# A hybrid encoder layer on one core: the next pair's columns move to another buffer, the down sums move to slots 13 to 46, and the last passes' outputs leave their banks in two steps

## The reference

```
h = rms(x); q, k, v, c = split(h @ w_in)
attn = window_attention(rms(q), rms(k), v)          # 128-query blocks, 384-key bands
u = a * sigmoid(gate); u = silu(layernorm(dwconv31(u)))
x = x + concat(attn, u) @ w_out
h2 = rms(x)
g = silu(dwconv3(h2 @ ffn_w_gate) + b)
x = x + (g * (h2 @ ffn_w_up)) @ ffn_w_down          # the larger part of the time
```

## Time and profile before

| what | value |
| --- | --- |
| median of 3 runs | 2567.1 us (2565.86 to 2567.85) |
| profiled execution, its own time | 2563.86 us |
| its span in the trace | 2561.8 us |
| PE busy | 2519.3 us, 98% of the span |
| DVE, ACT, POOL busy | 76%, 56%, 12% |
| DMA share in 0 to 200 us, 200 to 400 us | 0.94, 0.88 |
| granted PE clock, mean | 0.995 |

### The profile page before, as it was taken

The page is one execution under the profiler, slowest core; times in us unless marked ns, Lnnn a source line. Parts: engine busy times, 40 slices in busy tenths (PEclk is TensorE's granted clock), DMA queues, the critical chain, the costliest instruction groups (busy, mean ns, idle before and its releaser), DMA issues. The chain is left out here.

```text
span 2561.8 us, 36076 instructions
## 1 busy us (share of the span) xinstructions
PE 2519.3 (98%) x12663; PEld 2242.3 (88%) x12663; DVE 1936.6 (76%) x3228; ACT 1431.1 (56%) x2578; POOL 319.8 (12%) x483
## 2 busy tenths in 40 slices
PE   8999999999999999999999999999999899999997
PEld 7877777788878888888888899999999899999997
DVE  5886767887878697969794678687687887867864
ACT  6345544468436852784474356665655665655654
POOL 1110121201011102110101101100100111011011
PEclk9999999999999999999999999999999999999999
DMA  9988988834464456445537736735746675475465
GB/s 361 387 315 313 339 329 347 305 113 169 175 236 144 148 217 244 154 152 217 203 132 295 261 98 154 174 106 132 171 108 182 145 160 127 113 170 133 111 151 108
DMA packets 166834, 505.80 MB, mean 197 GB/s; under 512 B 28832, under 2 KB 37536, under 8 KB 147200
## 3 DMA queue, kind: packets, MB, share of 16 engines
q1 hardware_dynamic: 119344, 336.60, 37.6%
q0 software_dynamic: 47312, 166.91, 24.4%
HBM read 350.07 MB, written 153.36 MB: 197 GB/s over the span
## 5 line engine op out<-in xcount | busy, mean ns | idle before, releaser
L2037 DVE TENSOR_TENSOR part_lo<-part_raw,part_hi 128x512 fp32r<-128x512 f32 x462 | 316.7, 689 | 237.1 <-ACT part_hi L1561 234.3
L2357 PE MATMUL bank<-hw_hi,weights 128*128 128x462 f32 (+3 forms) x1408 | 420.7, 373 | 0.0
L1858 DVE SCALAR_TENSOR_TENSOR cc<-win,par,cc 128x512 f32<-128x512 f32 x600 | 408.3, 744 | 0.0
L1561 ACT ACTIVATE part_hi<-part_raw 128x512 fp32r<-128x512 f32 x462 | 285.7, 628 | 176.2 <-DMA part_raw<-w_pass_t 71.1
L2308 PE MATMUL bank<-h_hi,weights 128*128 128x512 f32 x1104 | 355.6, 395 | 0.0
L2521 PE MATMUL bank<-mid,part_hi 128*128 128x414 f32 x1232 | 337.3, 354 | 13.7 <-DVE pair_y L2122 6.0
L2357 PEld LDWEIGHTS bank<-hw_hi,weights 128*128 128x128 f32 x1408 | 264.7, 188 | 37.3 <-issue 12.2
L2357 PE MATMUL bank<-hw_lo,weights 128*128 128x464 f32 (+3 forms) x704 | 259.2, 368 | 0.0
L2308 PEld LDWEIGHTS bank<-h_hi,weights 128*128 128x128 f32 x1104 | 207.9, 188 | 51.7 <-issue 6.1
L2521 PEld LDWEIGHTS bank<-mid,part_hi 128*128 128x128 f32 x1232 | 231.9, 189 | 20.5 <-DVE part_lo L2037 9.9
L2503 PE MATMUL bank<-T_hi,part_hi 128*128 128x414 f32 (+1 forms) x704 | 246.0, 349 | 2.1 <-DVE e L2061 2.1
(11 more groups left out here) (231 smaller groups left out, 4596.1 us busy)
## 6 DMA issues: line engine op xcount, KB each, us to landing
weights<-weight_scratch SPq DMA_DIRECT2D x88, 1024.0 KB, 7.3
y_pair_t<-pair_y POOLq DMA_DIRECT2D x140, 414.0 KB, 7.8
wraw<-w_ffn_t SPq DMA_DIRECT2D x88, 512.0 KB, 3.3
part_raw<-w_ffn_t SPq DMA_DIRECT2D x176, 256.0 KB, 2.8
weight_scratch<-weights POOLq DMA_DIRECT2D x22, 1024.0 KB, 8.0
wraw<-w_down_t SPq DMA_DIRECT2D x44, 512.0 KB, 3.3
part_raw<-down_sums SPq DMA_DIRECT2D x88, 256.0 KB, 4.5
part_raw<-w_pass_t SPq DMA_DIRECT2D x66, 256.0 KB, 5.9
```

The source lines that it names most:

```text
L1561: nc.scalar.activation(p_hi[k % HI_RING][:], p_raw[part_of(k)][:], ACT.Copy).then_inc(s_whi, 1)
L1858: nc.vector.scalar_tensor_tensor(acc, win[i][:, tap:tap + TB], w_tap, acc, ALU.mult, ALU.add).then_inc(s_cv, 1)
L2037: nc.vector.tensor_tensor(p_lo[part_of(k)][:], p_raw[part_of(k)][:], p_hi[k % HI_RING][:].bitcast(F32), ALU.subtract).then_inc(s_wlo, 1)
L2357: mm = nc.tensor.matmul(out, l[:, k, :], r[:, k, cols], start=(k == 0 and j == 0), stop=(k == KT - 1 and j == 2))
```

## The change

It has three parts. First, the down sums' rounds start at slots 13, 16, 19, 23, 26, 29, 33, 36, 39, 43 and 46, where before they started at 12, 16, 20 and so on to 52. DVE's sums stand three slots later (16 to 49, before 15 to 55). Second, B12 of the next pair is loaded into the buffer of T2's hi part and no longer into that of T3. That load is released by product 6 instead of 7, the sum of T3 waits for product 7, and T2's hi part, which overwrites the columns, waits for the third of the window sums, which is T3's. Third, the outputs of the last pass leave in two steps: outputs 0 to 2 at the end of the list of row k, and output 3 at the front of the list of row k+1, where all four stood before.

```
-COMBO_AT = [12 + 4 * r for r in range(FT // 2)]
+COMBO_AT = [13 + 10 * r // 3 for r in range(FT // 2)]
...
-        if adds_sum(*PROD[_k][2:4]):
-            DVE_AT[_k + 1].insert(0, ("y_sum", _k))
+        _side, _op = (DVE_AT, "y_sum") if adds_sum(*PROD[_k][2:4]) else (ACT_AT, "y_copy")
+        if PROD[_k][2] == len(PASSES) - 1:
+            _side[_k].append((_op, _k, 0, KH - 1))
+            _side[_k + 1].insert(0, (_op, _k, KH - 1, KH))
         else:
-            ACT_AT[_k + 1].insert(0, ("y_copy", _k))
+            _side[_k + 1].insert(0, (_op, _k, 0, KH))
...
-        for _b, _p in (("B11", 1), ("B21", 2), ("B22", 3), ("B12", 7)):
+        for _b, _p in (("B11", 1), ("B21", 2), ("B22", 3), ("B12", 6)):
...
-        b_raw["B12"] = b_raw["T3"]
+        b_raw["B12"] = run(hi_at["T2"], ("B12_raw", [P, KH, B_PITCH], F32))[0][:, :, 0:TQ]
...
-                    sp.wait_ge(s_used, SLOTS + at(GROUPS * q - 1, {"B11": 1, "B21": 2, "B22": 3, "B12": 7}[b]) + 1)
+                    sp.wait_ge(s_used, SLOTS + at(GROUPS * q - 1, {"B11": 1, "B21": 2, "B22": 3, "B12": 6}[b]) + 1)
...
-                    act.wait_ge(s2_t, 4 * q + int(b[1]))
+                    act.wait_ge(s2_t, 4 * q + max(int(b[1]), 3 * (b == "T2")))
...
-            def pair_y_copy(k):
+            def pair_y_copy(k, first, last):
                 q, F, p = PROD[k][1:4]
-                for o, tile in y_outputs(k):
+                for o, tile in y_outputs(k)[first:last]:
...
-                if q > 0 and t != "T3":
-                    dve.wait_ge(s_used, SLOTS + at(GROUPS * q - 1, {"T1": 5, "T2": 6, "T4": 4}[t]) + 1)
+                if q > 0:
+                    dve.wait_ge(s_used, SLOTS + at(GROUPS * q - 1, {"T1": 5, "T2": 6, "T3": 7, "T4": 4}[t]) + 1)
...
-            def pair_y_sum(k):
+            def pair_y_sum(k, first, last):
                 q, F, p = PROD[k][1:4]
                 before = EVICTED[q, F, 2 if p == 1 else 3]
-                for o, tile in y_outputs(k):
+                for o, tile in y_outputs(k)[first:last]:
```

More of the change, by code:

```diff
@@ L1742, in _ @@
                     elif t[0] == "y_copy":
-                        pair_y_copy(t[1])
+                        pair_y_copy(*t[1:])
                     elif t[0] == "window_high":
@@ L2251, in _ @@
                     elif t[0] == "y_sum":
-                        pair_y_sum(t[1])
+                        pair_y_sum(*t[1:])
                     elif t[0] == "low":
```

## The result

The changed kernel took 2585.5 us in the median of 4 runs (2583.8 to 2589.2), the kernel before 2566.5 us: a ratio of 1.0076, with a 95% interval of 1.0059 to 1.0094, 19 us slower. The prediction was 2570 with a range up to 2577. It is wrong, and on the side of its rival "the combo buffer's chain becomes the bound", which it had priced at +9.7 us.

What follows compares the result with a forecast made beforehand. The prediction took PE as the bound, busy 2519.3 of 2561.8 us. Its terms, -3.8 + 3.5 + 0.5 + 2.6 = +2.8 us, on a median of 2567.1 gave 2570 us, range 2563.5 to 2577.

Steps and rivals of the forecast that it cites:

- the combo buffer's chain becomes the bound: Rival, chance 0.25: load, sums and store one after the other at 20.6 us make it slower, +9.7 us, 2577.
- The down sums: the rounds closer together: Rounds 20.6 or 27.4 us apart, before 27.4, make SP and sometimes DVE wait: +0.5 us, bounds 0 and +5.
- slot 49: Last round's four sums now stand ahead of `ln_acc`: longer PE stall and slow clock, +3.5 us, bounds +0.9 and +4.4.
- slot 55: Without the sums ahead of `qk` at 377 us, the stall (-2.1 us) and its slow clock (-1.7) go.
- faster: Rival, chance 0.15: early part gains 2.9 us and the late one is hidden, 2565, or 2561 without the 411 us stall.
- transfers short enough that no round waits: Rival, chance 0.05: with 4.7 us transfers a round takes 12.1 us and slot 49 costs nothing, -1.2 us, 2566.
- Between the pairs: Split outputs and T2's hi part waiting for T3's sum delay pair 1's start: +2.6 us, bounds +0.6 and +3.1.
- the gain without its last step: Lower end of the range, 2563.5 us: the early gain without the 411 us stall going as well.

Runs made afterwards that it cites:

- combo_last_late: The kernel before with only the last round's down sums and store one slot later (DVE slot 56), against the kernel before: ratio 0.9993 (0.9984 to 1.0002).

## Why the prediction was wrong

**The step that failed** is "The down sums: the rounds closer together", taken at +0.5 with bounds 0 and +5. With the term for slot 49 and the gain at slot 55 it made about 0; the slots alone measured +16 us. Three things in it were wrong.
- It asked whether DVE would be late, by the 4.0 us of the nearest `qk`. DVE's waits for its combo loads are small (7.9 us in 4 times with the slots alone). Who was late was SP, and the step named its waits and then only weight loads behind them. The loads of `xt` and `xs` behind the combo load have far less slack, and the `xt` loads feed ACT, which no step looked at. The kernel with two buffers shows the chain as the larger part.
- It compared a chain of 17.5 us with a distance of 20.6. But the chain's steps start at slots: the load waited for a store that stands one slot behind it. Waits of 9.3 us a round (84.1 in 9) came of this, 4.4 before (34.8 in 8). Putting the load at the store's own slot took SP's wait away and gave DVE one; both share one round that is too long.
- It priced the lower clock for one late `qk`. Here each of the three stalls of 3 to 5 us came with it, and of PE's 5.8 us more of busy time some 4.5 are its price.

**The rival "the combo buffer's chain becomes the bound"** had the place and the sign, with a chance of 0.25, and was priced at two stalls of 2 us, +7.4. There were three of 3.0, 4.9 and 4.2, the last of them in the place of slot 49. Its condition, a mean transfer over 8.9 us, was not met (mean 7.2 in the changed kernel, 7.4 before), and its reason, that closer rounds make the transfers slower, did not hold for them. It decided by the slots and not by the transfers' length; that the rival had the sign is so in part luck. The rivals "faster" and "transfers short enough that no round waits" fell. (The Trainium skill, "DMA: Bandwidth & Descriptors", section "Anatomy of one DMA — SWDGE (gpsimd) path", gives 2.0 us plus bytes over 436e3 for a transfer that POOL issues; an estimate by it is 4.4 us for a store of 1 MB. The trace agrees for the shortest store, 4.4, and not for the median, 8.6, at a DMA share of 0.81 to 0.87. The loads, which SP issues and to which the prediction applied it too, are not of that path.)

**Slot 55** was right in kind: in the changed kernel and in `combo_last_late` the 2.08 us stall and its slow clock are gone. The -3.8 us are not shown, as the timed runs of `combo_last_late` have 0.9993 with no change inside the interval. And "next late in this place is PE's own work, nothing" was wrong: with the sums away the same `qk` still waited 2.50 and 1.94 us in two kernels, for `kw`. **Slot 49** was right in place and wrong in cause: 4.20 us where 2.7 was taken and 3.56 was the most. `xs` did not land earlier, as I had hoped, but was waited for 11.49 us, 11.02 before. With two buffers the same sums stand there and the stall is 0.86 us, so the place is dear only while SP is held. The lower bound of +0.9 had that case.

**Between the pairs** mechanism and size were right, near the upper bound: +2.6 forecast with bounds up to +3.1, +3.05 measured with the old slots. Output 3 did undo the first step: PE waited 2.27 and then 1.9 us. The wait of T2's hi part costs little alone (+0.35), since T3's sum ends early enough; with the steps T3's sum is 2 us later and the split behind T2's hi part comes too late for DVE. That the parts' prices do not add, 0.35 and about 1 against 3.05, stands on single traces and stays open, as the timed runs say otherwise.

**The stall length.** The prediction took 2 us as roughly where the lower clock starts. The runs give no such line (last section). **The range.** Its lower end, 2563.5, is called the gain without its last step, which the rival's own sum puts at 2564.8; it changes nothing here.

## What to carry to other kernels

A wait on a DMA queue's engine is paid by whatever is queued behind it, however unrelated; before moving a load that waits for a store, list the loads behind it in that queue and who needs them. With one buffer, compare the distance of rounds with the whole round counted in program slots (load, use, store), and see that no load stands ahead of the store it waits for. Small waits behind an engine that is 98% busy are not all alike: a long one can bring the lower clock, which in the changed kernel cost some 1.5 us for 3 us of work at it. One trace of each kernel does not settle a gain of 3 us: the same lists put the same instruction up to 8 us apart.

## What was not expected of the hardware

The wait of PE at row n-8 for weights that land late varied from 1.53 to 2.87 us between executions of kernels that are the same there. Behind the five waits of up to 1.83 us no lower clock followed there; behind 1.90, 2.13, 2.19, 2.27, 2.28 and 2.87 it did, behind 2.35 and 2.52 it did not. Elsewhere it is the same: 1.90 us at 411.63 before was followed by it, and 1.91, 2.03, 2.46 and 2.50 us at waits near 380 and 410 us in four other kernels were not. The length of the wait alone does not decide it. The timed runs of one and the same kernel before spread over 2560.2 to 2574.3 us.
